# Two scans of the first pair, one behind the other or eight steps apart

## The reference, cut to what matters

```python
m = jnp.where(strict, jnp.einsum('nbhik,nbhjk->nbhij', kb, k) * decay, 0.0)
rhs = jnp.concatenate([v * beta[..., None], kb * jnp.exp(gc)[..., None]], axis=-1)
sol = lax.linalg.triangular_solve(m + jnp.eye(c, dtype=m.dtype), rhs, left_side=True,
                                  lower=True, unit_diagonal=True)
...
def step(s, xs):
    v_new = u_n - jnp.einsum('bhik,bhkv->bhiv', w_n, s)
    o = jnp.einsum('bhik,bhkv->bhiv', qi_n, s) + jnp.einsum('bhij,bhjv->bhiv', qk_n, v_new)
    s = s * gl_n + jnp.einsum('bhik,bhiv->bhkv', ko_n, v_new)
    return s, o
```

## Time and profile before

| | |
|---|---|
| median of three runs | 3729.6 us (3699.59 to 3743.17) |
| profiled execution | 3737.83 us, its span 3735.7 us |
| mean granted clock of PE | 0.902 |
| busy: PE, PEld, DVE | 2948.7 us (79%), 1694.3 us (45%), 2457.3 us (66%) |
| busy: ACT, POOL | 1190.7 us (32%), 1229.4 us (33%) |
| moved by DMA | 1225.40 MB, 328 GB/s over the span |

### The profile page before, as it was taken

The page is one execution under the profiler, slowest core; times in us unless marked ns, Lnnn a source line. Parts: engine busy times, 40 slices in busy tenths (PEclk is TensorE's granted clock), DMA queues, the critical chain, the costliest instruction groups (busy, mean ns, idle before and its releaser), DMA issues.

```text
span 3735.7 us, 31423 instructions
## 1 busy us (share of the span) xinstructions
PE 2948.7 (79%) x9692; PEld 1694.3 (45%) x9692; DVE 2457.3 (66%) x5022; ACT 1190.7 (32%) x3445; POOL 1229.4 (33%) x1094
## 2 busy tenths in 40 slices
PE   7666569688889869878887789797688777777776
PEld 6655446455556425644552246454355322222222
DVE  4343579787676768767756878656666868645444
ACT  1211133433232314243323342432232323334333
POOL 0000022355333413333433444323344424434332
PEclk9788789899889979978999999878899989999998
DMA  4102278799989959988999999979999969999996
GB/s 153 57 1 79 68 289 313 286 367 361 387 354 408 408 225 364 375 320 323 396 419 420 402 396 378 386 261 364 372 388 404 405 234 418 380 420 420 418 420 281
DMA packets 183659, 1225.40 MB, mean 328 GB/s; under 512 B 21185, under 2 KB 21585, under 8 KB 48194
## 3 DMA queue, kind: packets, MB, share of 16 engines
q0 software_dynamic: 153088, 1115.26, 74.6%
q1 hardware_dynamic: 30402, 108.12, 7.7%
HBM read 1211.46 MB, written 11.84 MB: 327 GB/s over the span
## 4 chain that ended last, share of the span: by engine, by line
PE 34%; DMA 30%; DVE 23%; issue 4%; ACT 4%; DVEq 3%; POOL 1%; SPq 0%; ACTq 0%; POOLq 0%
PE ps L475 33%; DMA ring<-in_uv,picked 29%; DVE ring L1824 6%; DVE otok L1783 2%; ACT scratch L908 2%; POOL ring L460 1%; DVEq L1645 1%; DVE scratch L1675 1%; DVE scratch L1649 1%; DVE scratch L1680 1%; DVE scratch L1651 1%; ACT diag L908 1%; DVE scratch L1655 1%; DVE scratch L1647 1%; DVE ids L1682 1%
## 5 line engine op out<-in xcount | busy, mean ns | idle before, releaser
L475 PE MATMUL ps<-ring,diag 128*128 128x512 f32 (+1 forms) x3380 | 1759.1, 651 | 459.8 <-ACT diag L908 449.2
L460 POOL DMA_INDIRECT ring<-in_uv,picked x1024 | 1162.8, 1136 | 2014.8 <-PE ps L475 1358.7
L1824 DVE SCALAR_TENSOR_TENSOR ring<-ring,htok 128x1024 f32<-128x1024 f32 x1024 | 1248.9, 1227 | 650.5 <-DMA ring<-in_uv,picked 643.6
L475 PEld LDWEIGHTS ps<-ring,diag 128*128 128x128 f32 (+1 forms) x3380 | 626.3, 201 | 1332.7 <-ACT diag L908 793.2
L908 ACT ACTIVATE act_v<-pre 128x1 f32<-128x1 f32 x1040 | 210.4, 202 | 1895.0 <-DVE ring L1824 1894.2
L475 PE MATMUL ps<-hT,wring 128*128 128x256 f32 (+1 forms) x3200 | 747.4, 389 | 59.3 <-DVE hT L1191 27.5
L475 PEld LDWEIGHTS ps<-hT,wring 128*128 128x128 f32 x3200 | 620.8, 194 | 233.8 <-issue 99.8
L908 ACT ACTIVATE diag<-masks,gated 128x128 f32<-128x128 f32 x829 | 332.8, 401 | 29.2 <-PE ps L475 2.1
L908 ACT ACTIVATE gated<-act_v,gates 128x1 f32<-128x1 f32 x1024 | 301.7, 295 | 33.3
L475 PE MATMUL ps<-scratch 128*128 128x128 f32 (+4 forms) x1424 | 241.3, 318 | 83.3 <-ACT scratch L908 32.3
L475 PEld LDWEIGHTS ps<-scratch 128*128 128x128 f32 (+2 forms) x1424 | 208.8, 213 | 160.6 <-issue 67.9
(11 more groups left out here) (243 smaller groups left out, 1624.4 us busy)
## 6 DMA issues: line engine op xcount, KB each, us to landing
wring<-in_weights SPq DMA_DIRECT2D x200, 512.0 KB, 7.8
ring<-in_uv,picked POOLq DMA_INDIRECT x1024, 11.4
scratch<-in_keys POOLq DMA_DIRECT2D x4, 1024.0 KB, 12.3
scratch<-in_s_gla POOLq DMA_DIRECT2D x4, 1024.0 KB, 12.1
out_o_gla<-scratch POOLq DMA_DIRECT2D x4, 1024.0 KB, 12.5
xT<-in_xT SPq DMA_DIRECT2D x1, 2080.0 KB
scratch<-in_s_dn POOLq DMA_DIRECT2D x1, 2048.0 KB, 9.5
scratch<-in_s_ssm POOLq DMA_DIRECT2D x1, 2048.0 KB, 15.0
```

Source lines behind the costliest of these rows:

```text
L460: pool.indirect_dma_start(out=ring[:, g % RING, :], out_offset=None, in_=io["uv"][L], in_offset=bass.IndirectOffsetOnAxis(ap=index, axis=0 ...
L475: return pe.matmul(out, lhsT, rhs, start=start, stop=stop)
L1824: stt(x, x, 1.0, h, MUL, MUL, accum_out=pre[:, g % SMALL:g % SMALL + 1]).then_inc(sem("dotted"), 1)
```

## The change

The first pair's two scans run side by side. On PE, ACT and DVE `side_by_side` takes step v of the first scan and then step v - 8 of the second (`SKEW` = 8). The two scans have their own temporaries: scan 1 has its own in the gathers' ring, the others in `scratch`. They have their own semaphores (a suffix 0 or 1) and their own PSUM banks: `SCAN_BANKS` names five for each scan, A, B, C, E and G; G is used for the decays as columns alone. To fit into them, the SSM transposes of x move from level 3 to level 5 on PE, behind a new wait, and their two products on DVE from step 21 to step 27, with a small copy `d_end` of the last column of `dec` before `dec` is overwritten. The second pair's scans (n = 2, 3) stay one behind the other, with the new bank numbers, the moved steps and the copy. The wait for the state (`even_group`) of scan n moves from step 0 to step 29 (n = 1) or is done at both (others). GpSimd's six masked copies keep their order, all of the first scan, then all of the second.

```diff
+SKEW = 8
...
+        def scan_temps(sc):
+            return [sc.take(12, P), sc.take(12, P)] + [sc.take(4, P) for _ in range(11)] + \
+                [sc.take(4, 512), sc.take(2, P), sc.take(12), sc.take(12), sc.take(12), sc.take(4), sc.take(8)]
+        temps = (scan_temps(Region(scratch, SCRATCH)),
+                 scan_temps(Region(ring[:, :, :].rearrange("p r d -> p (r d)"), RING * 2 * D)))
+        SCAN_BANKS = ((0, 1, 2, 3, 7), (4, 5, 6, 7, 3), (2, 3, 4, 5, 6))
...
         def even_scan(n):
-            return lambda off: even_slot(n // 2, E_SCAN + E_SCAN_LEN * (n % 2) + off)
+            return lambda off: even_slot(1, E_SCAN + E_SCAN_LEN * (n % 2) + off) if n > 1 else off
+
+        def side_by_side(scan):
+            first, second = Strand(scan(0)), Strand(scan(1))
+            for v in range(E_SCAN_LEN + SKEW + 1):
+                first.upto(v)
+                second.upto(v - SKEW)
...
@@ GpSimd
-                        pool.wait_ge(sem("n_ready"), n + 1)
-                        if 6 * n + l > 4:
-                            pool.wait_ge(sem("vt_mm"), 6 * n + l - 4)
+                        pool.wait_ge(sem(f"n_ready{q}"), m + 1)
+                        if 6 * m + l > 4:
+                            pool.wait_ge(sem(f"vt_mm{q}"), 6 * m + l - 4)
...
@@ PE, scan_even(n)
+                q, m = n % 2, n // 2
+                A, B, C, E, G = SCAN_BANKS[min(n, 2)]
...
-                pe.wait_ge(sem("even_group"), n + 1)
+                if n != 1:
+                    pe.wait_ge(sem("even_group"), n + 1)
...
                     if l == 2:
                         for j in range(2):
-                            mm(ps[:, 5, j * P:(j + 1) * P], col(16 + j), col(18 + j))
+                            mm(ps[:, E, j * P:(j + 1) * P], col(16 + j), col(18 + j))
                         for j in range(2):
-                            pe.transpose(ps[:, 5, 256 + j * P:256 + (j + 1) * P], col(16 + j), ident)
-                    if l == 3:
+                            last = pe.transpose(ps[:, E, 256 + j * P:256 + (j + 1) * P], col(16 + j), ident)
+                        last.then_inc(sem(f"ssm_mm{q}"), 1)
+                    if l == 5:
+                        pe.wait_ge(sem(f"ssm_done{q}"), 2 * m + 1)
                         for b in range(4):
-                            last = pe.transpose(ps[:, 6, b * P:(b + 1) * P], col(12 + b), ident)
-                        last.then_inc(sem("ssm_mm"), 1)
+                            last = pe.transpose(ps[:, E, b * P:(b + 1) * P], col(12 + b), ident)
+                        last.then_inc(sem(f"ssm_mm{q}"), 1)
...
                 yield slot(29)
-                pe.wait_ge(sem("wt_ready"), n + 1)
+                pe.wait_ge(sem(f"end_copied{q}"), 2 * m + 1)
+                pe.wait_ge(sem("even_group"), n + 1)
...
@@ PE, ACT and DVE, even(p)
-                for i in range(2):
-                    yield from scan_even(2 * p + i)
+                if p == 0:
+                    side_by_side(scan_even)
+                else:
+                    for i in range(2):
+                        yield from scan_even(2 * p + i)
...
@@ DVE, scan_even(n)
                     if l == 3:
                         yield slot(21)
-                        dve.wait_ge(sem("ssm_mm"), n + 1)
-                        cp(btk, ps[:, 5, 256:512].rearrange("p (a b) -> p a b", a=2))
-                        tt(xd8, ps[:, 6, :].rearrange("p (h c) -> p h c", h=8), bc(d_n, 64), MUL)
-                        dve.drain()
-                        tt(xo8, xd8, at_end(dec[:, 4:12, :]).to_broadcast([P, 8, 64]), MUL)
+                        dve.wait_ge(sem(f"ssm_mm{q}"), 2 * m + 1)
+                        cp(btk, ps[:, E, 256:512].rearrange("p (a b) -> p a b", a=2))
+                        cp(d_end, at_end(dec[:, 4:12, :]).rearrange("p h a -> p (h a)"))
...
+                        last.then_inc(sem(f"ssm_done{q}"), 1)
...
+                    if l == 5:
+                        yield slot(27)
+                        dve.wait_ge(sem(f"ssm_mm{q}"), 2 * m + 2)
+                        tt(xd8, ps[:, E, :].rearrange("p (h c) -> p h c", h=8), bc(d_n, 64), MUL)
+                        dve.drain()
+                        tt(xo8, xd8, bc(d_end, 64), MUL).then_inc(sem(f"ssm_done{q}"), 1)
```

More of the change, by code:

```diff
@@ L501, in scan_even @@
                 slot = even_scan(n)
+                q, m = n % 2, n // 2
+                A, B, C, E, G = SCAN_BANKS[min(n, 2)]
+                (dec, erow, nmat, qkt, kbt, kout, vb, pmat, xmat, vt, qi, xd, xo, nl, btk, eend, gct, egc, b_e, d_end) = temps[n == 1]
+                kb, wt, vn = vt, vt, xmat
                 at = 128 * (n % 2)
@@ L539, in scan_even @@
-                last.then_inc(sem("x0_ready"), 1)
+                    last = pe.transpose(ps[:, E, h * P:(h + 1) * P], pmat[:, h, :], ident)
+                last.then_inc(sem(f"setup_mm{q}"), 1)
                 yield slot(10)
                 for h in range(4):
-                    last = pe.transpose(ps[:, 4, h * P:(h + 1) * P], col(8 + h), ident)
-                last.then_inc(sem("kk_ready"), 1)
+                    last = pe.transpose(ps[:, C, h * P:(h + 1) * P], col(8 + h), ident)
+                last.then_inc(sem(f"setup_mm{q}"), 1)
@@ L569, in scan_even @@
                         if l == 1:
[L570 removed]
+                            pe.wait_ge(sem(f"setup_done{q}"), 3 * m + 3)
                         for h in range(4):
[L572 to L573 removed]
+                            last = mm(ps[:, C, h * P:(h + 1) * P], pmat[:, h, :], vt[:, h, :])
+                        last.then_inc(sem(f"z_mm{q}"), 1)
@@ L1288, in scan_even @@
                 slot = even_scan(n)
+                q, m = n % 2, n // 2
+                A, B, C, E, G = SCAN_BANKS[min(n, 2)]
+                (dec, erow, nmat, qkt, kbt, kout, vb, pmat, xmat, vt, qi, xd, xo, nl, btk, eend, gct, egc, b_e, d_end) = temps[n == 1]
+                kb, wt, vn = vt, vt, xmat
+                xd8, xo8 = [v.rearrange("p b (a c) -> p (b a) c", a=2) for v in (xd, xo)]
                 at = 128 * (n % 2)
@@ L1328, in scan_even @@
+                cp(xmat, bank4(E)).then_inc(sem(f"px_ready{q}"), 1)
                 yield slot(11)
-                dve.wait_ge(sem("kk_ready"), 4 * n + 4)
-                tt(vb, bank4(4), bc(b_n, P), MUL).then_inc(sem("vb_ready"), 1)
+                dve.wait_ge(sem(f"setup_mm{q}"), 6 * m + 6)
+                tt(vb, bank4(C), bc(b_n, P), MUL).then_inc(sem(f"setup_done{q}"), 1)
                 for l in range(1, LEVELS):
                     yield slot(11 + 3 * l if l < LEVELS - 1 else 28)
-                    dve.wait_ge(sem("z_mm"), 6 * n + l)
-                    last = tt(pmat, pmat, bank4(3), SUB)
+                    dve.wait_ge(sem(f"z_mm{q}"), 6 * m + l)
+                    last = tt(pmat, pmat, bank4(B), SUB)
```

170 lines of the change are left out of this document (80 added, 90 removed).

## The result

The changed kernel took 3683.8 us (median of 6 runs, 3656.84 to 3695.82), the kernel before beside it 3726.58 (6 runs). The ratio is 0.9886, with a 95% interval of 0.9851 to 0.9922: 42.5 us less, between 29 and 56 by the interval. The forecast was 36.5 us less. The profiled execution has a span of 3694.0 us against 3735.7.

The account below looks back on a forecast made before the run. Bound by a serial head, then mostly by transfers and gather order. Earlier start 41.1 less longer second scan 4.0 gives 37.1, less 0.6 for GpSimd is 36.5 us; from the median 3729.6 to 3693 us, range 3668 to 3718.

Parts of the forecast that it names:

- The head is serial, its gain goes through whole: Before the first gather: no transfer or other work overlaps the first two scans, so the remainder moves forward by their gain.
- this stretch stayed at 3262 within 15 us: Sign to check: the time from the first gather to the end stays at 3262 us within 15 us.
- Where the second scan's levels begin: First pair: the second scan begins level 1 at 204.4 us, 41.1 us earlier than now.
- the first rival: First pair's scans: matrix clock rises before 176 us and never falls; gain 42 us, time 3688 us; chance 0.18.
- How long it then takes: First pair, from its level 1: the second scan needs 53.7 us instead of 49.7; a level of each scan costs 6.62 us.
- GpSimd beside DVE: First pair: one scan's mask products may meet the other's masking, at most 1.28 us at each of two places; 0.6 taken.
- The second pair at 0: Second pair: moved steps and the small copy lose or win -6 to +6 us; 0 taken.
- The clock rival: First pair's scans: with more queued work the matrix clock stays up; gain 42 us, time 3688 us; chance 0.18.
- Harder coupling: First pair's rounds: in-order queues make one scan's waits hold the other, 8.5 us a round; gain 27, time 3703; chance 0.20.
- the bound at 1.2 GHz: First pair's scans: the matrix engine at its low clock limits, ending 6 us later than now, 3736 us; chance 0.04.
- the scans would not overlap at all: First pair: a second-scan step needing the first scan's end would give the old time, 3730 us; chance 0.03.
- the gain is given back later: Gathers' stretch: loses 10 to 20 us through the moved steps; time 3708 us; chance 0.05.

Follow-up runs that it names:

- after_5: The changed kernel run once more, unchanged: 3677.36 us, ratio 0.9897 to the kernel before.
- rows_late: Against the changed kernel, the second scan's three row blocks are all issued at its step 3: first row block to last state update 109.6 us instead of 103.6.

## Why the prediction was right

**The head is serial, its gain goes through whole.** Right up to the first gather. The gathers began 40.05 us earlier, and the head was 40.6 shorter. From the last state update to the first gather it is 178.6 us in before and 179.9 after. Measured in runs, 42.5 us: against the mean of three heads of before the difference is 43.4, since the execution that I summed from had the shortest head of the three. Behind the first gather it is less sure. That this stretch stayed at 3262 within 15 us was a weak sign, since the kernel before gave 3232 twice more. In the mean of three profiles it is 19 us longer in the changed kernel; the runs (42.5 us less above and, by the ratio of 0.9897, 38 in after_5, each give or take 14) speak against a loss of 20 us and leave room for one of 10.

**Where the second scan's levels begin.** Forecast 41.1 us earlier than now. Measured 245.47 less 200.17, less the 0.72 by which the whole head started earlier: 44.6. This is the term that was mis-sized, by 3.5 us. The main cause is the clock between 168 and 180 us. I had the two row blocks and the beta block there at the lower level (beta rows done at 181.9, measured 176.95) and put the other case aside as the first rival. rows_late shows that the blocks themselves keep the clock up. The 181.9 was not a clean sum either: from 176.8, with 2.09 for the level's block, 0.7 for the copy and its hand-overs and 1.78 for each of three more blocks, it would be 184.9. In the kernel the beta rows stand behind only one of the two further blocks, which gives 183.2. The two later gaps of about 4 us, and the lower clock after them, came as forecast (0.82 at 180 to 184, 0.60 at 192 to 196, a block at 2.08).

**How long it then takes.** Forecast 53.7 us, measured 253.83 - 200.17 = 53.7. The rounds from the first scan's level 4 to its level 6 (201.71, 208.18, 215.69) took 6.5 and 7.5 us; forecast were 6.65 and 7.7. So the order on the queues and the size of a round are what was right here, and not only their sum. The state update in front of the second scan's last update is there. With 49.7 for the second scan in before, the gain of 37.1 becomes 44.6 - 4.0 = 40.6.

**GpSimd beside DVE.** 0.6 us was taken, 1.28 the price of one meeting. One such meeting lies on the path, L1332 with 1.15 us instead of 0.15. The masking itself, which was to wait, lost nothing; GpSimd waited for it. Two more meetings, two operations of 2.36 us in sum instead of 1.29 at 208 and the copy `d_end` with 0.77 instead of 0.16 at 201.91, are hidden behind DVE's waits. The larger cost of this kind was in both kernels and not in my sum: 2 us in each set-up.

**The second pair at 0.** Not contradicted: 1.0027 (0.9989 to 1.0065) for the moved steps and the banks in all four scans, without the overlap.

**Rivals.** The clock rival gave 42 us and the runs 42.5, but only one half of it is true: up before 176, and down again after the gaps. Its own terms (2.7 and 2.2 us on 36.5) give 41.4, without the one gather that it adds. The agreement in the sum is partly that of before's longer heads. Harder coupling (27 us) did not occur: rounds are 6.5 to 7.5 us. The matrix engine never became the bound at 1.2 GHz; the clock is 0.88 over the head. The share of three quarters that I gave for it does not come out of its sizes: by them (an estimate: 60 us of matmuls at the upper clock, 120 at the lower, 14.4 of waits and copies) the 91 us up to 258 are full once some 33 of them are at the lower clock. That the scans would not overlap at all did not occur, and that the gain is given back later is the open point above.

## What to carry to other kernels

In a serial stretch in which every engine waits for the next, a second independent chain in the same queues costs little as long as the blocks of one fit into the waits of the other. Write down the order of one round in each queue and follow it to what ends last (here the two updates on DVE: 6.6 us for two levels instead of 10.6), then do the same for the start of the second chain. Here both came within 4 us. What stands in the gaps also sets the matrix clock, for better in the gaps it fills and for worse in the new ones that a long set-up on another engine opens. If the chains share a buffer, the distance between them is part of the program's correctness: here 8 and 9 steps give right outputs and 12 do not. Take more than one profile of before: a sparse stretch may differ by 6 us between executions of one kernel, a sixth of the gain here.

## What was not expected of the hardware

- The same instructions one behind the other took 144.2, 150.6 and 149.6 us in three executions, at a granted clock of 0.80, 0.75 and 0.75. With 256 more records of useless matmuls in their gaps the clock was 0.92 and the stretch 137.0 us: adding work made it shorter.
- A vector operation on 4 columns took 1.14 us instead of 0.15 beside a GpSimd product on SBUF, so what a meeting costs does not follow the vector operation's own length. The operation of 1.76 us in front of it, begun before GpSimd's, lost nothing.
- The time from the first gather to the end differed by 30 us between three executions of the kernel before (3232.3 to 3261.9), and by 44 us over all the kernels here (up to 3276.0).
